# Two attentions of a decoder trunk: probabilities scaled on the vector engine, and turned by plain transposes instead of products with a diagonal

## The reference, cut to what matters

```python
s = jnp.einsum('nqhmd,nkhmd->nhmqk', qi, k) * DK_A ** -0.5     # mixer A: two maps m
p = masked_softmax(s, k_pos[None, :] <= pi[:, None])
a = p[:, :, 0] - lam * p[:, :, 1]
return jnp.einsum('nhqk,nkhe->nqhe', a.astype(v.dtype), v)
...
ob = gates[..., 0:1] * o_cmp + gates[..., 1:2] * o_sel + gates[..., 2:3] * o_win   # mixer B
```

## Time and profile before

| | |
|---|---|
| three timed runs | 2133.76, 2136.41, 2153.38 us (median 2136.41) |
| the profiled execution | 2139.66 us, span of its trace 2138.0 us |
| busy over the span | PE 1993.3 us (93%), DVE 889.2 us (42%), ACT 473.0 us (22%) |
| mean granted clock of TensorE | 0.881 of full speed |
| prompt attention | from 411 to 543 us of the span |
| sample attention | from 551 to 699 us |

### The profile page before, as it was taken

How to read it: one execution, slowest core, us unless ns; L and a number is a source line. 1 busy time by engine, 2 the same in 40 slices (tenths; PEclk the granted TensorE clock), 3 DMA queues, 4 the chain that set the end, 5 groups by cost and what they waited for, 6 DMA issues and landing times.

```text
span 2138.0 us, 31164 instructions
## 1 busy us (share of the span) xinstructions
PE 1993.3 (93%) x13443; PEld 1786.5 (84%) x13443; DVE 889.2 (42%) x1628; ACT 473.0 (22%) x730; POOL 78.4 (4%) x146
## 2 busy tenths in 40 slices
PE   5989999899999789999999899988898899999998
PEld 3857778668788689999999888866677899999997
DVE  3533332245211356454544674223322564535352
ACT  1512130144322231111111324211111321111111
POOL 1000013200110000000000000000000000000000
PEclk7999999599765799999999999975556899999999
DMA  9566645300231122322224345211102212222221
GB/s 356 199 218 211 228 133 160 131 1 1 73 106 40 46 75 81 97 78 78 88 88 145 97 150 189 96 42 42 42 23 104 79 61 96 80 78 78 90 67 45
DMA packets 160173, 218.72 MB, mean 102 GB/s; under 512 B 7271, under 2 KB 131198, under 8 KB 159630
## 3 DMA queue, kind: packets, MB, share of 16 engines
q1 hardware_dynamic: 148814, 177.52, 25.2%
q0 software_dynamic: 11264, 39.86, 5.4%
HBM read 199.66 MB, written 21.76 MB: 104 GB/s over the span
## 4 chain that ended last, share of the span: by engine, by line
PE 88%; DVE 7%; ACT 2%; issue 1%; DMA 1%; SPq 0%; ACTq 0%; DVEq 0%
PE ps L1313 13%; PE ps L1315 13%; PE ps L1312 13%; PE ps L1023 4%; PE ps L1024 4%; PE ps L1025 4%; PE ps L1211 4%; PE ps L898 2%; PE ps L1124 2%; PE ps L1278 2%; PE ps L1110 2%; PE ps L1281 2%; PE ps L1279 2%; PE ps L1413 2%; PE ps L1427 2%; PE ps L1428 2%
## 5 line engine op out<-in xcount | busy, mean ns | idle before, releaser
L1312 PE MATMUL ps<-arena_r,wring_r 128*128 128x288 f32 x2048 | 569.4, 293 | 10.1 <-DVE hbuf_r L1994 10.1
L1315 PE MATMUL ps<-arena_r,wring_r 128*128 128x288 f32 x2048 | 434.9, 293 | 0.0
L1312 PEld LDWEIGHTS ps<-arena_r,wring_r 128*128 128x128 f32 x2048 | 386.4, 189 | 10.4 <-issue 10.4
L1315 PEld LDWEIGHTS ps<-arena_r,wring_r 128*128 128x128 f32 x2048 | 330.0, 189 | 0.0
L1313 PE MATMUL ps<-hbuf_r,wring_r 128*128 128x288 f32 x1024 | 287.6, 297 | 0.0
L1313 PE MATMUL ps<-arena_r,wring_r 128*128 128x288 f32 x1024 | 285.3, 295 | 0.0
L1739 ACT ACTIVATE wring_r<-wring 128x2048 fp32r<-128x2048 f32 x64 | 122.6, 1918 | 619.1 <-DMA wring<-in_mlp_w 619.1
L1313 PEld LDWEIGHTS ps<-hbuf_r,wring_r 128*128 128x128 f32 x1024 | 194.5, 190 | 0.0
L1313 PEld LDWEIGHTS ps<-arena_r,wring_r 128*128 128x128 f32 x1024 | 192.4, 188 | 0.0
L2315 DVE SCALAR_TENSOR_TENSOR xbuf<-ps,mod,xbuf 128x288 f32<-128x288 f32 (+1 forms) x128 | 56.1, 480 | 242.8 <-PE ps L1315 242.8
L1023 PE MATMUL ps<-wring_r,xbuf_r 128*128 128x512 f32 x360 | 147.9, 411 | 0.0
(11 more groups left out here) (362 smaller groups left out, 2953.7 us busy)
## 6 DMA issues: line engine op xcount, KB each, us to landing
wring<-in_mlp_w SPq DMA_DIRECT2D x64, 1024.0 KB, 5.2
arena<-in_ada_w SPq DMA_DIRECT2D x40, 1024.0 KB, 6.1
wring<-in_even_w_in SPq DMA_DIRECT2D x14, 1024.0 KB, 7.9
wring<-in_gla_w_in SPq DMA_DIRECT2D x12, 1024.0 KB, 5.4
wring<-in_ada_w SPq DMA_DIRECT2D x4, 2048.0 KB, 28.0
xbuf<-xspill SPq DMA_DIRECT2D x2, 2304.0 KB, 8.7
arena<-in_cache_cmp_kv POOLq DMA_DIRECT2D x16, 256.0 KB, 10.1
wring<-in_cache_diff_k POOLq DMA_DIRECT2D x16, 256.0 KB, 3.0
```

Of the source, the lines that this page charges most:

```text
L1312: pe.matmul(bank, hi, x_hi[:, k, cols], start=k == 0, stop=False)
L1315: mm = pe.matmul(bank, lo, x_hi[:, k, cols], start=False, stop=k == KC - 1)
```

## The change

VectorE no longer makes a diagonal matrix. It multiplies the probabilities by their factors in place, over all W columns, and in A the second map's instruction also adds the first map, which has been scaled before. TensorE then turns one finished matrix with plain transposes: t+1 for a group of A as of B, 3 for a unit of the sample attention. The semaphores `diag_ready` and `sdiag_ready` become `p_scaled` and `sp_scaled`; the wait of VectorE for a free diagonal buffer goes away, and the second map's step gets one more small instruction (1/sum times -lam) and a wait for the first map's scaling on its own engine.

```diff
             def p_turn(v):
...
-                pe.wait_ge(diag_ready, v + 1)
+                pe.wait_ge(p_scaled, v + 1)
...
-                both = [v - 1, v] if h < HA else [v]
                 for kb in range(t + 1):
-                    for u in both:
-                        mm = pe.matmul(ps[:, 3 + w % 2, kb * P:(kb + 1) * P], pbuf[:, u % 3, kb * P:(kb + 1) * P], diag[:, u % 3, :],
-                                       start=u == both[0], stop=u == v)
+                    mm = pe.transpose(ps[:, 3 + w % 2, kb * P:(kb + 1) * P], pbuf[:, v % 3, kb * P:(kb + 1) * P], ident[:, :])
                 mm.then_inc(pt_mm, 1)
...
             def s_turn(v):
-                pe.wait_ge(sdiag_ready, v + 1)
+                pe.wait_ge(sp_scaled, v + 1)
...
-                    mm = pe.matmul(ps[0:m, 5, b * P:(b + 1) * P], pbuf[:, v % 3, b * P:b * P + m], diag[:, v % 3, :], start=True, stop=True)
+                    mm = pe.transpose(ps[0:m, 5, b * P:(b + 1) * P], pbuf[:, v % 3, b * P:b * P + m], ident[:, :])
...
             def p_exp(v):
...
-                    act.wait_ge(diag_ready, v - 3)
+                    act.wait_ge(p_scaled, v - 3)
...
             def p_factor(v):
                 step(dve.reciprocal(rsum[:, v % 4:v % 4 + 1], sums[:, v % 4:v % 4 + 1]))
-                if v >= 3:
-                    dve.wait_ge(pt_mm, group_of[v - 3] + 1)
-                if h < HA:
-                    f = lam[:, 5:6] if b else ones[:, 0:1]
+                r, p = rsum[:, v % 4:v % 4 + 1], pbuf[:, v % 3, 0:(t + 1) * P]
+                if h >= HA:
+                    c = 3 * (h - HA) + 1 + b
+                    ins = dve.tensor_scalar(p, p, r, gates[:, t, c:c + 1], ALU.mult, ALU.mult)
+                elif b == 0:
+                    ins = dve.tensor_scalar(p, p, r, None, ALU.mult)
                 else:
-                    c = 3 * (h - HA) + 1 + b
-                    f = gates[:, t, c:c + 1]
-                dve.tensor_scalar(diag[:, v % 3, :], ident[:, :], rsum[:, v % 4:v % 4 + 1], f, ALU.mult, ALU.mult).then_inc(diag_ready, 1)
+                    step(dve.tensor_tensor(r, r, lam[:, 5:6], ALU.mult))
+                    dve.wait_ge(p_scaled, v)
+                    ins = dve.scalar_tensor_tensor(out=p, in0=p, scalar=r, in1=pbuf[:, (v - 1) % 3, 0:(t + 1) * P], op0=ALU.mult, op1=ALU.add)
+                ins.then_inc(p_scaled, 1)
...
             def s_factor(v):
...
-                if v >= 3:
-                    dve.wait_ge(spt_mm, v - 2)
-                dve.tensor_scalar(diag[:, v % 3, :], ident[:, :], rsum[:, v % 4:v % 4 + 1], None, ALU.mult).then_inc(sdiag_ready, 1)
+                p = pbuf[:, v % 3, 0:PAST + TS]
+                dve.tensor_scalar(p, p, rsum[:, v % 4:v % 4 + 1], None, ALU.mult).then_inc(sp_scaled, 1)
```

More of the change, by code:

```diff
@@ L240, in decoder_program @@
         pbuf = c2(3, 512)
-        diag = c2(3, P)
         ptb = Carve(mixer_scratch + 2 * (2 * SEQ + CL))(3, 512)
@@ L390, in decoder_program @@
         p_ready = sem("p_ready")
-        diag_ready = sem("diag_ready")
+        p_scaled = sem("p_scaled")
         pt_mm = sem("pt_mm")
@@ L404, in decoder_program @@
         sp_ready = sem("sp_ready")
-        sdiag_ready = sem("sdiag_ready")
+        sp_scaled = sem("sp_scaled")
         spt_mm = sem("spt_mm")
```

## The result

The changed kernel takes 2161.53 us (median; 2152.97 to 2168.01) against 2138.89 (2133.76 to 2153.38): a ratio of 1.0089, 95% interval 1.007 to 1.0107. That is 19 us slower by the ratio (23 by the medians), clear of noise, and outside the predicted range. Its profiled execution took 2160.23 us (span 2158.5; the kernel before: span 2138.0).

A forecast was written before the change was run, and what follows sets the result against it. TensorE's work was taken to bound both attentions. A +6.4, B -9.0 and sample -0.4 gave -3.0 us on the profiled 2139.66, 2136.7, rounded to 2136; range 2126 to 2148, eight in ten 2112 to 2156.

The forecast's parts named there:

- the sum: Prompt attentions A and B plus sample attention: -3.0 us on the profiled 2139.66 gives 2136.7, rounded to 2136.
- A +6.4: Prompt attention A, four heads: -0.6 for the first, +8.8 for two at low clock, -1.85 for the other.
- B -9.0: Prompt attention B, four heads: 40 turn records a head become 20, -2.25 us each.
- sample -0.4: Sample attention: shorter turns, but 6 of 11 units fast instead of 9; some 2.3 us saved in five other units.
- The low clock lasts: Rival: no clock rise in attention A and none in the sample units; +20 us, 2160; chance 0.18.
- What TensorE saves: Attention turns: a transpose is half a diagonal product, 0.1125 us a record at full clock; 320 records become 120.
- VectorE's step: Attention A: scalar-tensor-tensor takes 0.35, 0.48, 0.62, 0.75 us for the four widths; TensorE waits 2.03 us a head.
- The clock in A: Attention A: clock rises only shortly before B; two of the other three heads low, +4.4 us each.
- the forecast's 19.5 for a whole low head: Attention A, head at 1.2 GHz: 11.2 us without waits, +7.8 for slower streaming, 0.56 of wait left.
- The rival with two records for a transpose: Attentions: a transpose issues two records, so only A's doubled products are saved, none in B; about 2147; chance 0.03.

The follow-up runs named there:

- A alone: The change in attention A only, against the kernel before; attention B and the sample attention keep their diagonal products: 2166.71 us, ratio 1.0122.
- the shorter body: The changed kernel with 16 of the 768 products of an MLP loop's body left out and 32 waiting instructions at the start: 2118.83 us in one execution.

## Why the prediction was wrong

**The step that failed is the sum.** "A +6.4, B -9.0, sample -0.4: -3.0 us on the profiled 2139.66" has terms for the attentions alone. It takes for granted that everything behind them costs what it did, and 496 instructions fewer in front of a loop is a change to that loop. Its term was +23 us in the profiled execution. The page before showed the queue that carries it (70 packets of code), and no term rests on it.

**The rival that gave 2160 was not right.** "The low clock lasts" hits the measured time by chance: in the traces of the changed kernel and of A alone attention A took as long as before, and in that of the changed kernel the sample was shorter. Its term for A was real, though: in one of five executions with single transposes (the shorter body) A was low throughout and took 75.2 us, 12.7 more than before, where the rival had 12.6. A total that fits says nothing about a mechanism; the stage table does.

**What TensorE saves** was sized well. The turns have 120 records where they had 320, as forecast, and the chain of the kernel after gives the heads; L2164 here is the sum on DVE for the last tile of each head of A, L1135 the last values of a head of B:

```profile
428.90 0.76 DVE arena L2164
...
448.84 0.76 DVE arena L2164
...
463.59 0.76 DVE arena L2164
...
476.54 0.76 DVE arena L2164
...
492.60 0.89 PE ps L1135 x8
...
506.76 0.89 PE ps L1135 x8
```

A head of A at the low clock takes 19.94 us (forecast 19.5), at the full clock 12.95 (13.2), a head of B 14.16 (14.0). From B's first score product to the sample's first key turn it is 68.5 us instead of 77.2: B gained 8.7 of the 9.0.

**VectorE's step** was right to the hundredth: the scalar-tensor-tensor takes 0.35, 0.48, 0.62 and 0.75 us, from the maxima's slope and one row of another stage. TensorE waits for it, 2.16 us in the third head of A, the one wholly at the full clock (forecast 2.03), and now the chain of A runs through DVE. The tensor-scalar of B takes 0.55 for 512 columns, and costs B 0.6 us of PE's time:

```profile
L1121 PE MATMUL ps<-cf,arena 128*128 128x128 f32 x120 | 24.7, 308 | 6.0 <-DVE arena L2164 5.4 <-DVE arena L2158 0.6
...
L2164 DVE SCALAR_TENSOR_TENSOR arena<-arena,rsum 128x512 f32<-128x512 f32 x4 | 3.0, 750 | 0.1
...
L2158 DVE TENSOR_SCALAR arena<-arena,rsum,gates 128x512 f32<-128x512 f32 x8 | 4.4, 546 | 0.3
```

**The clock in A** went the forecast way and not as far. One later head was wholly low and one half, not two. By their first score products the heads changed by -3.3, +4.9, +0.1 and -2.0 us: A came to -0.3 instead of +6.4. The first head was sized wrongly. From its first turn to that of the next head it took 20.14 us before and 18.27 after (416.46 to 434.73), so it gained 1.9 and not 0.6: the forecast's 19.5 for a whole low head holds the last values of the head before, 1.71 us at the low clock, and no head stands before the first.

```profile
416.46 0.44 PE ps L1121
...
435.13 1.71 PE ps L1135 x8
```

The clock takes A's gain: with single transposes the low stretch lasted 37.5 us in four executions and all of A's 75 us in a fifth; with all or half of them doubled 13.7 (three) and 23.9, and A took 56.5 to 58.2 and 62.1. With the old products it lasted 12 to 20 us in four executions.

**The sample** came to -2.1 instead of -0.4. Its eleven units took 101.8 us where 101.9 were forecast, and that is luck: three were fast, not six, but fast ones took 7.41 us, not 8.15, and slow ones 9.95, not 10.6. Nor is -2.1 a figure of the edit: in five other executions of its sample code the stage took 142.1 to 152.5 us, in four of the old code 151.7 to 154.4.

**A sum that doesn't come out.** The rival with two records for a transpose counts 40 records for the doubled products of A; they are 40 products, 80 records, and its terms don't lead to 2147. Nothing else rests on it.

So the attentions gave -11 us where -3 was forecast. The changed kernel with its code moved has a ratio of 0.9935, which is 2122.5 on the median 2136.41 (2115 to 2130 by its interval): 13 us under the forecast, below its own range (2126 to 2148) and inside that for eight in ten (2112 to 2156). So the attentions' terms were off too, but by less than the missing one. The +5 us of the first loop belong to executions, not to the change.

## What to carry to other kernels

An edit that adds or removes instructions moves all code behind it on that engine (shown here for TensorE); where a loop follows, count its body against the 16 KB packets in which code arrives, and compare the instruction queue's packets before and after. If a stage that an edit doesn't touch gets slower, look at the loop's jump back for idle time that ends with "issue", and test it with a few instructions that do nothing. Work taken from TensorE beside waits can lose in clock what it saves, so look for its price by issuing part of it twice.

## What the chip showed that was not expected

By the count of theory 1, a loop whose code touches seven packets was fetched once in four passes. One that touches eight was fetched again behind each of the second loop's three jumps, in four kernels, and behind two of the first loop's three jumps in a fifth: nine packets and 5.5 to 6.9 us of idle TensorE a jump. The Trainium skill (Runtime: NRT & Kernel Launch, Instruction fetch mechanics) says that TensorE's code buffer is a FIFO of 128 KiB, refilled in blocks of 16 KiB with 256 instructions, and that a taken branch whose target isn't in the current window of two pages stalls for a fetch. The packets of 16 KB and the stalls at the jumps agree; the window of two pages does not, for the seven-packet loop jumps back over some six packets and was fetched once for four passes. An estimate from the 128 KiB of the Trainium skill (the same section) is eight blocks held, by which seven and one ahead would stay and eight and one ahead would not; no run here varies the buffer, so that reason isn't shown.

The MLP's products start every 131.67 ns in most executions of the loops, and every 130.0 ns throughout the first loop in some, at the same granted clock: 5 us of 406. What sets it was not tried.

Waiting instructions on TensorE that are satisfied at once cost 21 us for 256, 0.08 us each; forty in an idle stretch cost nothing that shows.
